# Packing the two heads of a step side by side in the TensorE array, and writing the head loop out without staging copies

## What is computed

```python
# latent heads: q, k have 96 columns (64 + 32 with rotary), v has 64
sc = einsum('bqhd,bkhd->bhqk', qb, k) * scale;  sc = where(causal, sc, -inf)
o_a = einsum('bhqk,bkhd->bqhd', softmax(sc), v) * silu(gate_a)
# sparse heads: q, k, v have 64 columns; 8 query heads share 2 key/value heads;
# only the top 128 keys of an index score count for a query
sc = einsum('bqkgd,bqjkd->bqkgj', qg, kg) * scale
o_b = einsum('bqkgj,bqjkd->bqkgd', softmax(sc), vg) * silu(gate_b)
merged = sigmoid(m_a + b0) * (o_a @ w_branch_mla) + sigmoid(m_b + b1) * (o_b @ w_branch_dsa)
x = x + merged @ w_out
```

## Time and profile before

| | us |
|---|---|
| Median of 3 runs | 1381.68 |
| Profiled execution, its time | 1377.67 |
| Profiled execution, its span (first to last instruction) | 1375.9 |
| PE busy | 1319.2 (96%) |
| VectorE (DVE) busy | 701.8 (51%) |
| ScalarE (ACT) busy | 635.1 (46%) |
| GpSimd (POOL) busy | 101.5 (7%) |
| Mean granted TensorE clock | 0.984 of full |

### The profile page before, as it was taken

The page is one execution under the profiler, slowest core; times in us unless marked ns, Lnnn a source line. Parts: engine busy times, 40 slices in busy tenths (PEclk is TensorE's granted clock), DMA queues, the critical chain, the costliest instruction groups (busy, mean ns, idle before and its releaser), DMA issues.

```text
span 1375.9 us, 16463 instructions
## 1 busy us (share of the span) xinstructions
PE 1319.2 (96%) x5984; PEld 1057.5 (77%) x5984; DVE 701.8 (51%) x1176; ACT 635.1 (46%) x926; POOL 101.5 (7%) x215
## 2 busy tenths in 40 slices
PE   6999999999999997999999999999868999999999
PEld 5787877878777786788888888878656777777887
DVE  5445444544444453542443524453698888435671
ACT  5645455563556552431322313354725545545830
POOL 1000010100001010000000000000121111111000
PEclk9999999999999999999999999999987999999999
DMA  5322212122221224132222322243111233533611
GB/s 200 104 69 96 69 65 84 57 95 69 95 69 65 99 60 158 51 114 81 91 91 95 102 108 91 91 134 116 62 61 39 100 122 104 185 116 130 244 62 61
DMA packets 26531, 134.42 MB, mean 98 GB/s; under 512 B 3320, under 2 KB 4408, under 8 KB 13696
## 3 DMA queue, kind: packets, MB, share of 16 engines
q1 hardware_dynamic: 16992, 107.49, 22.4%
q0 software_dynamic: 4896, 17.03, 3.8%
q10 hardware_dynamic: 4608, 9.44, 1.8%
HBM read 121.35 MB, written 11.55 MB: 97 GB/s over the span
## 4 chain that ended last, share of the span: by engine, by line
PE 89%; DVE 5%; ACT 3%; DMA 2%; issue 1%; POOL 0%; DVEq 0%; ACTq 0%; POOLq 0%
PE proj L291 71%; PE pa L1331 2%; PE pm L1288 1%; DMA x_res<-in_x 1%; PE pm L1338 1%; PE pa L1295 1%; PE pm L1451 1%; PE pa L1451 1%; PE pa L1288 1%; PE pa L1433 1%; PE pm L1433 1%; PE pa L1308 1%; PE pm L1443 1%; DVE rope L1048 1%; PE pm L1317 1%
## 5 line engine op out<-in xcount | busy, mean ns | idle before, releaser
L291 PE MATMUL proj<-h_hi,w_hi 128*128 128x512 f32 x960 | 385.6, 402 | 2.6 <-ACT sq_q L551 1.7
L291 PE MATMUL proj<-h_hi,w_lo 128*128 128x512 f32 x960 | 375.0, 391 | 0.0
L291 PE MATMUL proj<-h_lo,w_hi 128*128 128x512 f32 x960 | 374.7, 390 | 0.0
L264 DVE TENSOR_TENSOR w_lo<-w_raw,w_hi 128x2048 fp32r<-128x2048 f32 x100 | 228.0, 2292 | 151.9 <-ACT w_hi L258 149.7
L258 ACT ACTIVATE w_hi<-w_raw 128x2048 fp32r<-128x2048 f32 x100 | 189.8, 1911 | 147.0 <-PE proj L291 140.2
L291 PEld LDWEIGHTS proj<-h_hi,w_hi 128*128 128x128 f32 x960 | 181.0, 189 | 45.0 <-issue 7.0
L291 PEld LDWEIGHTS proj<-h_hi,w_lo 128*128 128x128 f32 x960 | 180.7, 188 | 38.7
L291 PEld LDWEIGHTS proj<-h_lo,w_hi 128*128 128x128 f32 x960 | 180.9, 188 | 38.4 <-issue 2.9
L291 PE MATMUL proj<-w_hi,act_hi 128*128 128x512 f32 x256 | 99.6, 389 | 0.0
L291 PE MATMUL proj<-w_hi,act_lo 128*128 128x512 f32 x256 | 99.6, 389 | 0.0
L291 PE MATMUL proj<-w_lo,act_hi 128*128 128x512 f32 x256 | 99.6, 389 | 0.0
(11 more groups left out here) (362 smaller groups left out, 1866.2 us busy)
## 6 DMA issues: line engine op xcount, KB each, us to landing
w_raw<-in_wall SPq DMA_DIRECT2D x100, 1024.0 KB, 5.1
gates<-gate_st ACTq DMA_DIRECT2D x24, 256.0 KB, 2.0
m_all<-gates POOLq DMA_DIRECT2D x2, 1536.0 KB, 8.3
x_res<-in_x ACTq DMA_DIRECT2D x4, 512.0 KB, 6.3
bc<-gate_rows POOLq DMA_DIRECT2D x8, 256.0 KB, 3.4
x_res<-in_x POOLq DMA_DIRECT2D x1, 2048.0 KB, 12.8
x<-x_res POOLq DMA_DIRECT2D x1, 2048.0 KB, 7.2
g_all<-gates POOLq DMA_DIRECT2D x1, 2048.0 KB, 14.4
```

The lines of the kernel that those rows point to most:

```text
L264: nc.vector.tensor_tensor(w_lo[:, slot, 4 * half:4 * half + 4, :], w_raw[:, half], w_hi[:, slot, 4 * half:4 * half + 4, :], ALU.subtract)\
L291: mm = nc.tensor.matmul(proj[:, bank, :], lhsT, rhs, start=(k == 0 and q == 0), stop=(k == kts - 1 and q == 2))
```

## The change

- The loops over c and b become written-out Python loops; step numbers are constants.
- The GpSimd copies to `q_st`, `k_st` and `v_st` go. Transposes and pv read q, k and v where they lie. What stays on GpSimd is four copies that write each of the two sparse key heads twice, side by side (`k_dup`), once for all sparse steps.
- pv of both heads goes to `pa`: head 0 uses 64 stationary columns and writes partitions 0 to 63, head 1 writes partitions 64 to 127; the matmuls of the heads alternate. One copy of 128 partitions takes both out.
- In a sparse step, four 128-column transposes turn q of both heads at once (head 0 on rows 0 to 63 of `qT[0]`, head 1 on rows 64 to 127). k is turned once for steps 4 to 7. Scores of the two heads alternate, on rows 0 to 63 and rows 64 to 127 of the array, to `pa` and `pm`.
- The turn of q for the next sparse step stands ahead of pv (that of step 4, and the turn of k, in step 3), and the scores stand right behind pv of the step before; both gates 0 and 1 then lie between scores and pT. Scores of i = 3, which write the bank that pv used, wait for the output copy.
- In each pair, head 1 goes before head 0.
- The first load of `m_all` takes 5 of its 16 parts instead of 6, the second 5 instead of 4.

```diff
-            def head_turn(u, B, d):
-                t_.wait_ge(S[f"staged{u}"], 2 * B + 2)
-                t_.wait_ge(S[f"o_sb{u}"], B + 1)
+            def latent_turn(u, B):
+                if u == 0 and B:
+                    t_.wait_ge(S["o_sb"], B)
...
+            def sparse_turn_q(B):
+                t_.wait_ge(S["pT_sb1"], B)
+                for t in range(TB):
+                    mm = t_.transpose(pm[:, 1024 + P * t:1024 + P * (t + 1)], q_b2[:, t, P * (B - 4):P * (B - 3)], ident[:, :])
+                mm.then_inc(S["qk_turned0"], 1)
...
+            def sparse_scores(B):
+                t_.wait_ge(S["qk_sb0"], 5 + B)
+                t_.wait_ge(S["qk_sb1"], 8 + KV_D)
+                k = kT[(B - 4) // 2]
+                for i in (2, 0, 1, 3):
+                    if i == 3:
+                        t_.wait_ge(S["o_sb"], B)
+                    for u, X in enumerate((pa, pm)):
+                        r = slice(D_D * u, D_D * (u + 1))
+                        mm = t_.matmul(X[:, LOW[i]:LOW[i] + P * (i + 1)], qT[0][r, P * i:P * (i + 1)],
+                                       k[r, 0:P * (i + 1)], start=True, stop=True)
...
-            def head_pv(u, B):
-                X = (pa, pm)[u]
-                t_.wait_ge(S[f"pT_sb{u}"], B + 1)
-                t_.wait_ge(S[f"v_staged{u}"], 2 * B + 2)
+            def head_pv(B):
+                for u in range(2):
+                    t_.wait_ge(S[f"pT_sb{u}"], B + 1)
                 for i in range(TB):
-                    mm = t_.matmul(X[:, P * i:SEQ], v_st[u][:, i, :], pT[u][:, TRI[i]:TRI[i] + SEQ - P * i],
+                    for u in range(2):
+                        c = D_D * (2 * B + u) if B < 4 else D_D * ((B - 4) // 2)
+                        mm = t_.matmul(pa[D_D * u:D_D * (u + 1), P * i:SEQ], (v_a2 if B < 4 else v_b2)[:, i, c:c + D_D],
+                                       pT[u][:, TRI[i]:TRI[i] + SEQ - P * i], ...
...
+            for B in range(4, 8):
+                sparse_scores(B)
+                gate(B, B % 2, 0)
+                gate(B, B % 2, 1)
+                head_pT(1, B)
+                head_pT(0, B)
+                gate(B, B % 2, 2)
+                if B < 7:
+                    sparse_turn_q(B + 1)
+                head_pv(B)
```

More of the change, by code:

```diff
@@ L181, in program @@
         p_sb = [at(f"p_sb{u}", (60 + 14 * u) * K, [P, TRI_COLS]) for u in range(2)]
[L182 to L184 removed]
+        k_dup = [at(f"k_dup{i}", (65 + 16 * i) * K, [P, TB, P]) for i in range(KV_D)]
         gate_st = at("gate_st", 83 * K, [P, 2, SEQ])
@@ L445, in _ @@
                     .then_inc(S["ka_gained"], 1)
[L446 to L492, removed]
@@ L494, in _ @@
-            gp.wait_ge(S["v_staged0"], 16)
-            gp.wait_ge(S["v_staged1"], 16)
+            gp.wait_ge(S["idx_done"], 1)
+            for i in range(TB):
+                x = idx[:, LOW[i] + P * i:LOW[i] + P * (i + 1)]
+                gp.affine_select(out=x, in_=x, compare_op=ALU.is_ge, fill=NEG, base=0,
+                                 pattern=[[-1, P]], channel_multiplier=1).then_inc(S["idx_causal"], 1)
+            gp.wait_ge(S["rope"], 6 * 15)
+            gp.memset(causal[:, :], 0.0).then_inc(S["causal0"], 1)
@@ new lines, in _ @@
+            gp.wait_ge(S["causal0"], 1)
+            gp.affine_select(out=causal[:, 384:512], in_=causal[:, 384:512], compare_op=ALU.is_ge, fill=NEG,
+                             base=0, pattern=[[-1, P]], channel_multiplier=1).then_inc(S["causal_made"], 1)
+            for i in range(KV_D):
+                for w in range(2):
+                    gp.tensor_copy(k_dup[i][:, :, D_D * w:D_D * (w + 1)], k_b2[:, :, D_D * i:D_D * (i + 1)])\
+                        .then_inc(S["k_dup"], 1)
+            gp.wait_ge(S["pv"], 4)
@@ L785, in gate @@
                     .then_inc(S[f"gates_stored{q}"], 16)
[L787 to L806, removed]
+            for B in range(4):
+                c, s = B // 2, B % 2
+                split_hi(G_L + B + 1, s, 0, used=T_L + 3 * B)
+                latent_turns(1, B)
+                latent_turns(0, B)
+                gate(c, s, 0)
+                head_exp(1, B)
+                head_exp(0, B)
+                split_hi(G_L + B + 1, s, 1, used=T_L + 3 * B)
+                gate(c, s, 1)
+                head_pT(1, B)
+                head_pT(0, B)
+                gate(c, s, 2)
+                if B == 3:
+                    sparse_q(4)
+                    sparse_k()
+                a.wait_ge(S["o_stored"], 16 * B + 16)
+                head_out(B, o_st[:, :])
+                a.wait_ge(S["o_sb"], B + 1)
+                a.dma_start(o_d[bass.ds(B, 1)].rearrange("a p n -> p (a n)"), o_st[:, :]).then_inc(S["o_stored"], 16)
             for B in range(4, 8):
@@ L1165, in top @@
                     v.match_replace(x, top8[:, i - 1, :], x, TAKEN).then_inc(S["top_out"], 1)
[L1167 to L1177, removed]
+            for B in range(4):
+                split_lo(G_L + B + 1, B % 2, 0)
+                for u in (1, 0):
+                    head_max(u, B, lambda i: causal[:, 384 - P * i:512], QK_M ** -0.5)
+                head_norm(1, B)
+                head_norm(0, B)
+                split_lo(G_L + B + 1, B % 2, 1)
+                for rnd in range(4):
+                    top(B, rnd)
             v.wait_ge(S["top_out"], 49)
@@ L1432, in head_scores, with sparse_turn_k @@
                 for i in range(TB):
-                    mm = t_.matmul(X[:, LOW[i]:LOW[i] + P * (i + 1)], qT[u][0:d, P * i:P * (i + 1)],
-                                   kT[u][0:d, 0:P * (i + 1)], start=True, stop=True)
+                    mm = t_.matmul(X[:, LOW[i]:LOW[i] + P * (i + 1)], qT[u][0:QK_M, P * i:P * (i + 1)],
+                                   kT[u][0:QK_M, 0:P * (i + 1)], start=True, stop=True)
                 mm.then_inc(S[f"scores{u}"], 1)
+            def sparse_turn_q(B):
[3 more added lines that the diff above has]
+                mm.then_inc(S["qk_turned0"], 1)
+            def sparse_turn_k():
+                t_.wait_ge(S["k_dup"], 2 * KV_D)
+                t_.wait_ge(S["pT_sb1"], 4)
+                for i in range(KV_D):
+                    for t in range(TB):
+                        mm = t_.transpose(pm[:, 512 * i + P * t:512 * i + P * (t + 1)], k_dup[i][:, t, :], ident[:, :])
+                mm.then_inc(S["qk_turned1"], 1)
+            def sparse_scores(B):
[9 more added lines that the diff above has]
+                                       k[r, 0:P * (i + 1)], start=True, stop=True)
+                        if i == 3:
+                            mm.then_inc(S[f"scores{u}"], 1)
             def head_pT(u, B):
@@ L1455, in _ @@
-            for kind, d in enumerate((QK_M, D_D)):
-                with t_.Fori(0, 2) as b:
-                    for s in range(2):
-                        B = 4 * kind + 2 * b + s
-                        head_turn(0, B, d)
-                        head_turn(1, B, d)
-                        gate(B, s, 0)
-                        head_scores(0, B, d)
-                        head_scores(1, B, d)
-                        gate(B, s, 1)
-                        head_pT(0, B)
-                        head_pT(1, B)
-                        gate(B, s, 2)
-                        head_pv(0, B)
-                        head_pv(1, B)
+                    for u in range(2):
+                        c = D_D * (2 * B + u) if B < 4 else D_D * ((B - 4) // 2)
+                        mm = t_.matmul(pa[D_D * u:D_D * (u + 1), P * i:SEQ], (v_a2 if B < 4 else v_b2)[:, i, c:c + D_D],
+                                       pT[u][:, TRI[i]:TRI[i] + SEQ - P * i], start=(i == 0), stop=(i == TB - 1))
@@ new lines, in head_pv @@
+                mm.then_inc(S["pv"], 1)
+            t_.wait_ge(S["rope"], 6 * 11)
+            for B in range(4):
+                latent_turn(1, B)
+                latent_turn(0, B)
+                gate(B, B % 2, 0)
+                latent_scores(1, B)
+                latent_scores(0, B)
+                gate(B, B % 2, 1)
+                head_pT(1, B)
+                head_pT(0, B)
+                gate(B, B % 2, 2)
+                if B == 3:
+                    sparse_turn_q(4)
+                    sparse_turn_k()
+                head_pv(B)
```

71 lines of the change are left out of this document (37 added, 34 removed).

## The result

The changed kernel takes 1350.2 us (median of 4 runs, 1349.56 to 1354.22), the one before, beside it, 1381.68: a ratio of 0.978, with the interval 0.976 to 0.980. Once more on another chip it was 1349.27 (5 runs) against 1379.24 (15 runs), 0.979 (0.977 to 0.980): 30.0 us. The profiled executions are 1377.67 and 1349.56, 28.1 apart. The forecast was 1357.5, its range began at 1352: direction and mechanism as forecast, the gain 6 to 7 us larger.

What follows compares the result with a forecast made beforehand. PE was taken to bound the head loop. Latent steps 6.1 + sparse steps 20.5 - 0.9 - 0.2 - 1.3 = 24.2 us off 1381.68 gave 1357.5; own range 1353 to 1361, 1352 to 1372 with rivals.

Steps and rivals of the forecast that it cites:

- PE bounds the loop: Head loop from step 1: a microsecond off PE is one off the kernel, while other engines' chains stay shorter.
- pv 2.45: Every step: pv of both heads on column groups takes 2.45 us instead of 4.32.
- splits at 0.2 each: Head steps: each change of the array's row or column split costs PE about 0.2 us, 1.4 in the latent steps.
- strict order: Packed blocks: matmuls start strictly in program order, making pv 2.56 us and sparse scores 2.77.
- Sparse scores 2.25: Sparse steps: both heads' scores on row groups take 2.25 us, between 2.16 fully parallel and 4.32 in series.
- Rivals 1, 3 and 4: 1: only row groups parallel, 1371, chance 0.12; 3: neither packing parallel, 1379.4, 0.04; 4: pv weight loads exposed, 1395, 0.04.
- The removed GpSimd copies at nothing: Staging copies: removing them gains nothing, since they ran beside PE, which never waited for them, and POOL is 7% busy.
- One new wait at step 4 of 1.3: Step 4: PE waits 1.3 us, once, for VectorE's normalised weights at pT.
- 1.8 us to spare in steps 5 to 7: Second head's pT: weights ready at t + 12.9, wanted at t + 14.7, t being the end of the previous pv.
- rival 2: New waits for VectorE or ScalarE eat part of the gain, leaving about 17 us: 1365, chance 0.10.
- some 3.7 in each step: Sparse steps: without the moved gate, PE would stop for some 3.7 us in each.
- Written-out loops at nothing: Loops over c and b: writing them out costs or gains nothing, at most a fraction of a microsecond either way.

Runs made afterwards that it cites:

- e2: Changed kernel with both heads' pv matmuls on columns 0 to 63, summed there: 1365.05 us (0.990), pv 4.45 us a block.
- e1: Changed kernel with pv giving all four matmuls of head 0, then of head 1, still on two column halves: 1360.68 us (0.987).
- e3: Changed kernel with sparse scores giving all four matmuls of head 0, then of head 1, still on two row halves: 1351.79 us (0.981).
- e10: Kernel before without GpSimd staging copies, loops written out, m_all loads split as in the change: 1376.34 us against 1379.51 (0.998).
- e4: Changed kernel with both heads' sparse scores on rows 0 to 63, still alternating: 1356.59 us (0.984), 4.51 us a block.
- e6: Changed kernel with gate 0 of sparse steps ahead of the scores again: 1356.53 us (0.984).
- e7: Kernel before with its three head loops written out, nothing else: 1379.07 us against 1379.24 (1.000).
- e8: Changed kernel with both packings off, pv on the same columns and scores on the same rows: 1372.83 us against 1379.0 for the kernel before (0.995).
- e5: Changed kernel with VectorE's split_lo of the first weight half behind both head_norms in all eight steps: 1345.34 us (0.976).
- e9: Changed kernel with split_lo of the first half behind both head_norms, except ahead of head_max in steps 2 and 3: 1345.45 us against 1379.0 (0.975).

## Why the prediction was off, step by step

Its forecast lay 7.3 us above the time. 3.7 are in the loop (27.9 against 24.2), 1.6 ahead of it, and 2.0 is scatter: the median shown of before is 4.0 above its profiled execution and that of after 0.6. Against the 30.0 of the other chip the forecast gain is 5.8 short, and 0.5 of that is left for scatter.

1. **PE bounds the loop: right.** What PE saved in a step, the step saved.
2. **The term "pv 2.45" with splits at 0.2 each: the step that failed by its size.** The mechanism is as forecast (4.45 with both heads on the same columns in e2, 2.30 in the change), but the value was put between parallel and strict order, and it is parallel to 0.14. And 0.4 was added for the ways in and out of the split, read off from the 64-row scores. In a latent step both and the block come to 27.09 - (29.06 - 4.32) = 2.35 where 2.85 was taken, so the ways add 0.05 to the block and not 0.4. That is the 0.5 of each of steps 1 and 2. In steps 5 and 6 the pieces are 0.44 + 2.30 + 2.36 + 11.11 + 2.18 + 5.48, where 11.11 still has the way out of the scores (0.17 above two gates of 5.47), but no way in shows ahead of pv or of the scores: 0.4 less for the ways and 0.15 for pv, against 0.1 more for the scores. Over the eight steps the term makes 3.7 us; step 4's longer wait takes 0.4 of that back, and step 0's gate adds 0.3 (point 4).
3. **Sparse scores 2.25: right in kind, 0.1 low.** Strict order would have been 2.77. e1 and e3 give the rule that holds here: a matmul for a free part of the array may pass about three that stand before it. The index scores of the kernel before had shown the same three already: `pm` at 1010.62, ahead of `pa` at 1010.93, 1011.25 and 1011.68. The Trainium skill (page "TensorE: Matmul & The Clock Gate", section "Part 3: Packing small matmuls — row/col tiling") has matmuls in strict order of start and end. The trace does not agree: in e3 `pm` starts at 1187.53, ahead of `pa` matmuls at 1187.74 and 1187.96. In strict order only the last matmul of head 0 and the first of head 1 could have run together in e3, 384 columns or 0.32 us, some 4.2 a block; it has 3.33. Nor does a weight load hold up pv, though both tiles share their rows: 16 loads and 16 matmuls take 2.30. Rivals 1, 3 and 4 are out.
4. **"The removed GpSimd copies at nothing": the other step that failed.** The reason given was that PE never waited for them and POOL is 7% busy. Both are true and miss the point: the copies slowed VectorE where PE waits for VectorE, at the `idx` weighting and at the end of step 0. e10 prices it at 3.2 by the times and 2.5 by the trace. In the change it is the 1.6 ahead of the loop and 0.3 of what step 0 saved beyond its forecast (its gate took 5.95 before and 5.65 after, with a granted clock of 0.66 and 1.00 from 1069.7 to 1071). The Trainium skill (page "SBUF — State Buffer", section "Who interferes with whom") says that a two-port instruction of VectorE and a GpSimd instruction exclude each other for their whole length. The trace agrees that they hinder each other: 2.02 for 1.27 us. Whether these are two-port instructions, and whether one shuts the other out for its whole length, no run here shows.
5. **One new wait at step 4 of 1.3: right.** It was 1.66, step 4's 25.54 less the 23.88 of a step without it: 0.36 + 0.87 of waiting in its two rows, and the rest around them. It is also why a packing taken away costs less than its blocks (e2, e4).
6. **1.8 us to spare in steps 5 to 7: right.** VectorE had the second head's weights ready at 1198.46 in step 5, and PE began their pT at 1200.29. No wait appeared, so rival 2 is out, and e6 shows that without the moved gate there would be one in each step. But the "some 3.7 in each step" that the prediction gave for that was too much: it counted the gate's whole 5.47 as cover lost, but `split_lo` holds VectorE until t + 4.96 in any case, so with the gate ahead of the scores it starts only some 3 us later (5.47 + 2.45 - 4.96). e6 measured 1.78 in steps 5 and 6.
7. **Written-out loops at nothing: right** (e7). The copies of pT in step 7 came in time: the last ended at 1254.15 and pv began at 1254.55.

What stays open: why the granted clock falls in some executions ahead of the loop and not in others (part of the scatter of some 3 us), and the exact price of one change of the array's split, since no run isolates it. No run swaps the order of the two heads alone; in e8's loop, which has it, nothing is gained beyond the fewer turns.

## What to carry to other kernels

Two matmuls that each fill half of the array's rows or columns ran in little over half their time (2.36 for 4.51, 2.30 for 4.45), but only when given alternately: one after the other they kept 1.2 of 2.15 us in the rows and 0.6 of 2.15 in the columns. When PE sheds work, look at once at the softmax chain that it used to wait on: its place among the gates (e6, 7.3 us) and what else stands in VectorE's queue (e5 and e9, some 4 us) decided as much here as packing the scores (7.0). Before a copy on an idle GpSimd is costed at nothing, look at what VectorE does beside it, and who waits for that.

## What the runs showed of the hardware

- TensorE started a matmul for a free row group or column tile ahead of up to three earlier ones (the starts in e3 and e1; their blocks took 3.33 and 3.86 us, against 2.36 and 2.30 alternating and 4.51 and 4.45 in series).
- Two column tiles share rows and load their weights behind running matmuls: sixteen loads of 64 columns were hidden in 2.30 us.
- The same four VectorE instructions took 2.02 us beside GpSimd copies and 1.27 without.
